# Delta stage of a two-block network: unread TensorE products beside VectorE's sort, solve and spread

## What is computed

```
lmat  = where(i > j, (beta k) k^T * decay, 0)
sol   = triangular_solve(I + lmat, [beta v, beta k exp(gc)])
v_new = u - w S
S     = S * g_last + k_dec^T v_new
o     = (q exp(gc)) S + ((q k^T) * decay) v_new
```

## Time and profile before

| | us |
|---|---|
| median of 3 runs | 2783.12 |
| lowest, highest | 2774.38, 2784.1 |
| the profiled execution | 2786.81 |
| its span on the core | 2785.1 |
| delta stage in it | about 1189 to 1475 |

### The profile page before, as it was taken

One profiled execution on the slowest core, in us unless ns is written; L12 is line 12 of the kernel. 1 busy time (PEld: TensorE's weight loads), 2 busy tenths in 40 slices (PEclk: granted clock), 3 DMA queues, 4 the chain that ended last, 5 costly groups with the idle time before them and its releaser, 6 DMA issues. The chain is left out here.

```text
span 2785.1 us, 26506 instructions
## 1 busy us (share of the span) xinstructions
PE 2357.4 (85%) x11120; PEld 1536.2 (55%) x11120; DVE 687.3 (25%) x1504; ACT 447.5 (16%) x867; POOL 173.8 (6%) x238
## 2 busy tenths in 40 slices
PE   6975768879996799755898799999978769999997
PEld 5833655668883347345786454454437654445443
DVE  3474220122201221267621311111100221111112
ACT  1313111122101212231232100000001020000001
POOL 1042000011002000051000000000000000000000
PEclk9977889989996899675878899999978879999998
DMA  6310123224448320000004599999995339999993
GB/s 203 135 36 30 61 76 121 75 78 153 149 141 285 124 91 31 0 1 1 1 1 181 243 427 426 427 428 426 424 333 186 120 125 427 428 427 427 427 428 164
DMA packets 120018, 575.53 MB, mean 207 GB/s; under 512 B 5152, under 2 KB 28281, under 8 KB 95321
## 3 DMA queue, kind: packets, MB, share of 16 engines
q1 hardware_dynamic: 118431, 570.59, 51.3%
q0 software_dynamic: 768, 2.02, 0.3%
q10 hardware_dynamic: 698, 1.18, 0.1%
HBM read 572.72 MB, written 1.05 MB: 206 GB/s over the span
## 5 line engine op out<-in xcount | busy, mean ns | idle before, releaser
L415 PE MATMUL linear_ps<-hT,ring 128*128 128x256 f32 x1344 | 301.3, 388 | 39.0 <-PEq L334 18.3
L415 PEld LDWEIGHTS linear_ps<-hT,ring 128*128 128x128 f32 x1344 | 261.4, 195 | 78.9 <-issue 42.0
L2259 PE MATMUL ex_u<-ring_extra,ex_xt 128*64 128x512 f32 x1024 | 226.5, 596 | 6.7 <-DMA ring_extra<-in_w 6.7
L2259 PE MATMUL ex_u<-ring,ex_xt 128*64 128x512 f32 x1024 | 224.8, 593 | 4.9 <-DMA ring<-in_w 3.4
L1340 PE MATMUL dp_ps<-dn_src,ring 128*128 128x512 f32 (+1 forms) x512 | 168.1, 492 | 6.4 <-PEq L334 6.4
L2259 PEld LDWEIGHTS ex_u<-ring_extra,ex_xt 128*64 128x64 f32 x1024 | 76.5, 138 | 153.2 <-issue 153.2
L2259 PEld LDWEIGHTS ex_u<-ring,ex_xt 128*64 128x64 f32 x1024 | 77.7, 137 | 147.5 <-issue 147.5
L1073 PE MATMUL ffn_ps<-hT,ring 128*128 128x256 f32 x704 | 153.7, 382 | 5.9 <-PEq L334 5.9
L1073 PEld LDWEIGHTS ffn_ps<-hT,ring 128*128 128x128 f32 x704 | 134.8, 192 | 24.8 <-issue 6.3
L2348 DVE TENSOR_TENSOR ex_hid<-ex_sil,ex_u 128x512 f32<-128x512 f32 x32 | 34.7, 1084 | 437.0 <-PE ex_u L2259 437.0
L1340 PEld LDWEIGHTS dp_ps<-dn_src,ring 128*128 128x128 f32 x512 | 98.3, 192 | 76.3 <-issue 69.7
(11 more groups left out here) (442 smaller groups left out, 2819.5 us busy)
## 6 DMA issues: line engine op xcount, KB each, us to landing
ring<-in_w SPq DMA_DIRECT2D x96, 2048.0 KB, 23.9
ring_extra<-in_w SPq DMA_DIRECT2D x96, 2048.0 KB, 25.0
ring<-in_ada_w SPq DMA_DIRECT2D x24, 2048.0 KB, 17.9
ring<-in_ffn_w_up SPq DMA_DIRECT2D x22, 1024.0 KB, 6.4
ring<-in_w_in SPq DMA_DIRECT2D x8, 2048.0 KB, 9.0
ring<-in_w_in_a SPq DMA_DIRECT2D x8, 2048.0 KB, 13.2
ring<-in_w_in_b SPq DMA_DIRECT2D x6, 2048.0 KB, 18.0
ring<-in_ffn_w_down SPq DMA_DIRECT2D x5, 2048.0 KB, 8.0
```

What stands on the lines that cost most here:

```text
L415: mm = pe.matmul(ps[:, q % banks, 0:n], w[:, k, j * P:(j + 1) * P], src[:, k, 0:n], start=k == 0, stop=k == kc - 1)
L2259: mm = pe.matmul(u[H * a:H * a + H, i, :], xt[:, b, k, H * a:H * a + H], w[a][:, 512 * k:512 * k + 512], start=k == 0, stop=k == KC - 1, s ...
```

## The change

Four things are done to `stage_delta`, all on TensorE's side.

1. A helper issues products of 128x512 (identity times keys of head 0) into a PSUM bank that nobody reads at that time. They are put: two behind each of the four sort transposes of half 0; one behind the first operation of each of the 31 solve steps of half 0; one behind ScalarE's mix copy of either half; three behind each of the four spreads of half 0 and one behind each of half 1.
2. Each of these groups waits for a semaphore value of VectorE or ScalarE, so TensorE now keeps its place in the list. In particular the sums of fronts 5, 6 and 7 stand behind the products of the solve steps before them.
3. q k^T has one bank, 7, since bank 2 takes the unread products.
4. With it, the gram products of front h (h over 0) wait until VectorE has done L1893 of all heads before.

```
-        qk_ps = lambda h: ps[:, (7, 2)[h % 2], 0:T].rearrange("p (t n) -> p t n", t=TT)
+        qk_ps = lambda h: ps[:, 7, 0:T].rearrange("p (t n) -> p t n", t=TT)
...
+            def keep_going(n, bank):
+                for _ in range(n):
+                    pe.matmul(ps[:, bank, :], K.ident[:, :], kT[:, 0, :], start=True, stop=True)
+
             for what, h, k in delta_schedule():
                 g = h // HG
-                if what == "front" and h < NH:
+                if what == "turn" and h == 0:
+                    for b in range(4):
+                        pe.wait_ge(dl["sorted"].sem, dl["sorted"].at(b + 1))
+                        keep_going(2, 2)
+                elif what == "solve" and h == 0:
+                    pe.wait_ge(dl["solved"].sem, dl["solved"].at(2 * k + 1))
+                    keep_going(1, 2)
+                elif what == "mix":
+                    pe.wait_ge(dl["mixed"].sem, dl["mixed"].at(2 * h + 2))
+                    if h:
+                        pe.wait_ge(dl["high"].sem, dl["high"].at(2 * HG))
+                    keep_going(1, 3 if h else 2)
+                elif what == "spread":
+                    pe.wait_ge(dl["spread"].sem, dl["spread"].at(4 * h + k + 1))
+                    keep_going(1 if h else 3, 3 if h else 2)
+                elif what == "front" and h < NH:
...
+                    if h:
+                        pe.wait_ge(dl["gram_used"].sem, dl["gram_used"].at(2 * h))
                     for t in range(4):
                         pe.matmul(gram_ps(h)[:, t, :], kT[:, h, t * P:(t + 1) * P], kT[:, h, t * P:(t + 1) * P], start=True, stop=True)
```

## The result

The changed kernel takes 2801.35 us (median of four runs, 2799.78 to 2803.89) against 2783.09 us for the kernel before on the same chip: a ratio of 1.0073, with a 95% interval of 1.0052 to 1.0095. It is slower by 18.3 us where 25 were forecast. The time lies in the predicted range, 2788 to 2820, but not for the forecast's reasons alone: the waits cost some 28 us instead of 25, and heads 4 and 5 gave back 16.7 us where none was forecast.

The account below looks back on a forecast made before the run. VectorE was taken to bound the delta stage's solve, mix and spread, then TensorE at half clock. Costs 9.8 + 3 + 0 + 12 = 25 us gave 2808 against the median of 2783; range 2788 to 2820.

Parts of the forecast that it names:

- Part 1: First half's solve steps: sums of heads 5 to 7 wait behind unread products, delaying VectorE three times, 9.8 us together.
- The rival of half-clock products: Unread products in the solve run at half clock, some 12 us more, 2820 in all; chance 0.10.
- Part 2: Fronts ahead of the solve: with one qk bank, gram products wait for VectorE; 3 us, bounds 0 and 6.0.
- Part 3: First half's sort and spread: products hidden, TensorE then idle 4.8 us in head 0, clock falls; no gain for head 1.
- the row of 1250: Earlier profile's clock reading, 0.71 in 1250 to 1252, used to say the clock falls 4 to 6 us after TensorE stops.
- the prize: Gain from a high clock at the start: 10.2 us for head 1, 10.2 for head 5, perhaps 4 for head 4.
- The rival that the clock stays high through the hole: Clock stays high through head 0's 4.8 us idle time, head 1 and the second spread; 2780, not slower; chance 0.08.
- Part 4: Second half's mix and spread: TensorE's waits stand between head 3's chain steps; 12 us, 8.4 at full clock, 13.3 at half.
- the three short waits: After second-half spread blocks 1, 2 and 4: a product and a chain step, 1.3 us each at full clock, 2.2 at half.
- the one behind block 3: Second half's third spread block: "new" is held back, 5.7 us at half clock, 3.5 at full.
- Part 4's last sentence: Head 4, after the second half's spreads: enters at half clock as before, with no gain.
- the rival that had a chance of 0.20: Clock returns in the second half only; heads 4 and 5 at full clock give back 14 us, so 2794; chance 0.20.

Follow-up runs that it names:

- x1: The changed kernel without the 31 unread products of the solve steps and their waits; median 2788.14 us, ratio 1.0014.
- x5: The changed kernel with the sums of front h+1 issued right behind front h's products, ahead of the next solve steps' unread ones; 2798.38 us, ratio 1.0063.
- x4: The kernel before with only the single q k^T bank and the gram products' wait for VectorE, no unread product; 2790.18 us in one run.
- x12: The kernel before, unaltered, run and profiled a second time; 2782.86 us.
- x9: The changed kernel, unaltered, run and profiled a second time; 2800.04 us, ratio 1.0052.
- x6: The changed kernel with five more unread products, without a wait, behind head 0's first join; median 2798.10 us, ratio 1.0055.
- x8: The kernel before plus unread products at half 0's spreads, head 0's hole, and half 1's mix and (without a wait) spreads; none in sort or solve; 2767.07 us, ratio 0.9948.
- x11: x8 with two more unread products behind the first join of head 4; 2753.62 us, ratio 0.9887.
- x7: The changed kernel with three unread products, without a wait, at each second-half spread instead of one that waits; median 2797.66 us, ratio 1.0048.
- x2: The kernel before with the single q k^T bank, its wait and the 31 solve-step products; none at sort, mix or spread; 2800.22 us, ratio 1.0051.
- x3: The changed kernel without the five unread products and waits at the second half's mix and spreads; median 2790.14 us, ratio 1.0031.
- x10: The changed kernel with the solve steps' 31 unread products cut from 512 to 256 columns; 2793.49 us in one run.

## Why the prediction came out as it did

**Part 1, solve steps: 9.8 forecast, 12.9 measured.** The mechanism is right: x1 and x5 both give 34.0, and x5 shows that it is the sums behind the products. The step that was mis-sized is "they keep TensorE busy nearly without a gap, so I expect 1.00". The working had the gram products wait for VectorE's front, and that very wait, 2.73 us, is the gap that it left out. The clock over the solve steps was 0.89. The rival of half-clock products is true in part: about 3.1 us of its 12.

**Part 2, fronts: 3 forecast, 0.8 measured** (29.0 in the changed kernel and x4 against 28.2, or 1.3 against the 27.7 of x12). Near the lower bound. That GpSimd's queue hides the wait fits the prediction's reading, but no run tests it.

**Part 3: right.** The hole was put at 4.8 us and measured 4.84; the clock was expected to fall in it, and it fell to 0.50 by 1312; head 1 takes 28.1 us. The 4 to 6 us that the prediction read off the row of 1250 are no measure of it: in x9 the clock fell within a microsecond. x6, x8 and x11 give the other side: with the hole filled 11.4 us come back, where the prize had been put at 10.2. The rival that the clock stays high through the hole fell here. The rule of the Trainium skill that stood beside it (TensorE: Matmul & The Clock Gate, section on why this matters for your kernels: no idle gaps between bursts of matmuls) agrees with what x6 shows. It does not cover the other rows: TensorE was busy 4.00 of 4.00 us at 0.50 in x12 (1404.80), so gapless 128x64 products did not raise the clock there.

**Part 4: 12 forecast, 14.0 measured**: mix 1.1, the blocks 10.3, and 2.6 us of the wait behind the fourth block, which falls into the rest. That is a little over its upper end, 13.3. Each of the three short waits was priced at 2.2 for half clock and is 2.6; the one behind block 3 was priced at 5.7 and its wait is 4.51. x7 shows that the wait makes nearly all of it (9.8 us of the blocks).

**The step that failed is Part 4's last sentence,** that head 4 enters at half clock as before, with no gain. In the changed profile head 4's first products begin at 1416.66; the clock is back 1 us later and stays:

```profile
1414.70:1417.70 3.00, 2.98 (x15) 2.69 (x14) 0.70 (x2) 0.74 (x2) 0.00 (x0) 0.52 0.00 0
1417.70:1420.70 3.00, 3.00 (x29) 3.00 (x29) 0.00 (x0) 1.46 (x5) 0.00 (x0) 1.00 0.02 5
```

Head 5 gives back 10.2 us, exactly the prize; head 4 gives 6.5 and not 4. Of these 16.7 the late wait takes 2.6, which leaves 14.1, the figure of the rival that had a chance of 0.20. With it in place of no gain the forecast would have been 25 - 14 = 11 for the stage, and 11.6 is what the first pair of profiles shows: the larger waits (3.1 and 2.0 more) made up for the smaller fronts (2.2 less) and the larger give-back (2.7 more). The prediction had named this among its own signs of being wrong ("if heads 4 and 5 run at 1.00"). The medians moved by more, 18.3 us, and the second pair of profiles, whose rest before was 89.1, has 17.0 for the stage: there the give-back beyond the kernel before is 9.7 only. By its own mechanism, no gain, the waits as they were would have made 28 us, so 2811. The measured 2801.35 lies at the lower edge of the forecast's span (2801 to 2813) and just above the rival's (2788 to 2800); that it fell on the forecast's side is luck.

**What stays open: when a rise outlives head 4.** The rest by kernel:

| rest, us | kernels |
|---|---|
| 93.3 to 93.5 | before, x2, x3 (profiled run), x4 |
| 89.1 to 89.9 | before again (x12), x1, x5 |
| 85.6, 86.9 | x7, x8 |
| 79.4 | changed, x9, x6, x10 |
| 76.9 | x11 |

x5 and the changed kernel run the same products from the second mix on. In head 4 both have the same pause: after eight 64x64 records TensorE waits 0.68 us for ScalarE. In x5 the clock is 0.94 and then 0.50 behind it, in the changed kernel (last line) it stays:

```profile
1411.28 0.65 PE L1767 MATMUL dl_ps<-ring 64*64 64x64 f32 x8 [0.68 <-ACT ring L1881]
...
1412.30:1413.30 1.00, 1.00 (x12) 0.85 (x11) 0.62 (x2) 0.04 (x1) 0.00 (x0) 0.94 0.00 0
1413.30:1414.30 1.00, 1.00 (x8) 1.00 (x6) 0.23 (x1) 0.30 (x1) 0.00 (x0) 0.50 0.00 0
...
1424.75 0.65 PE L1761 MATMUL dl_ps<-ring 64*64 64x64 f32 x8 [0.69 <-ACT ring L1875]
```

What differs is when the stretch comes, some 13 us earlier in x5, and how long ahead of it the clock had risen: 5 us ahead of the product behind the pause in x5 (at 1406.3), 7 in the changed kernel (at 1417.6). In all four profiles with a rest of 79.4 the clock rose some 5 us behind the last spread, in x1, x5 and x12 some 8; in x7 and x8 it had been at 1.00 long before, and fell as well. So neither the rise nor the pause alone decides. Nor is it shown that the five unread products of the second half bring the give-back: x1 has them and a rest of 89.9, x12 has none and 89.1, and of x3, without them, only a long run was profiled (93.3). That the moment decides is a reading, not shown: no run moved this stretch by a few microseconds and left all else. What is shown is that the clock fell 1 to 3 us behind this pause in x1, x5, x7, x8 and x12, and that with two products in it (x11 against x8, which also put what follows some 0.5 us later) the clock stays and the rest goes from 86.9 to 76.9.

## What to carry to other kernels

Unread products paid here only where TensorE is idle and nobody waits for what stands behind them: 32 of them in the holes make this kernel 1.1% faster, 57 of them, some ahead of sums and chain steps that VectorE wants, make it 0.7% slower, though the clock rises in both. Put them behind, never ahead of, the next product that another engine needs, without a wait if the order around them already paces TensorE. And look for the last hole of the stretch: filling all but one of them brought nothing for head 1.

## What the runs showed of the hardware

- The granted clock dropped behind short idleness: behind 2.73 us without work in the solve, in head 0's hole of 4.8 us (some 4 us into it in one profile, within 1 us in the other), and in head 4 behind a pause of 0.68 us among 64x64 products in five profiles (x1, x5, x7, x8, x12), while four others (changed, x6, x9, x10) kept it there. How much idleness it takes these runs do not tell.
- Being busy alone did not bring it back: float32 products of 128x64, each with a 128x128 weight load, kept TensorE busy 4.00 of 4.00 us at 0.50 (x12), and 16.55 of 16.80 us in head 4 before. With the clock high the same work took 17.8 us instead of 28.0 (head 5) and 10.3 instead of 16.8 (head 4, at 0.95).
- The clock's changes can come at the same places in kernels that differ only ahead of them, and on two chips (79.4 us of rest in x6 on one, in x9 and x10 on another), but not always: before has 93.5 and 89.1 in its two profiles. A change that shortens one stretch by 13 us can lose 10.5 us in a later one that it does not touch (x5), so a gain in one stage is to be read in the stretches behind it too.
